# Half of the gate cells by accumulating scatters instead of one-hot products

## The chip, the cores and the metric

The kernel runs on one core of a Trainium2 chip. The metric is device time in microseconds, the median of several runs; before the change it is 2739.08 us (three runs, 2737.34 to 2743.43).

## What is computed

One encoder layer runs on two groups of tokens, 256 of the prompt and 512 of the sample (called the first and the second group here). Its attention and pooling half is not touched by the change. The other half is PEER, an expert retrieval over 128 x 128 = 16384 single-neuron experts:

```python
s = jnp.einsum('thpd,hpnd->thpn', q, keys)                 # 8 heads, 2 halves, 128 keys
top_s, top_i = lax.top_k(s, 16)
cand = top_s[:, :, 0, :, None] + top_s[:, :, 1, None, :]
best_s, best_j = lax.top_k(cand.reshape(128, 8, 256), 16)
expert = i1 * 128 + i2                                     # 16 experts per token and head
g = softmax(best_s)
act = gelu(einsum('thkd,td->thk', u[expert], x)) * g
out = einsum('thk,thkd->td', act, v[expert])
```

So each token uses 8 x 16 = 128 experts, each with a weight `g` (its gate).

## The kernel before

**Two ways of evaluating the experts.** For the second group (512 tokens, four blocks of 128) the kernel works densely. A first pass goes over the whole table `u` in 128 turns of 128 experts: TensorE multiplies a tile of `u` with all 512 tokens (`score`, 24 matmuls of 512 columns, because each operand is split in a high and a low part), ScalarE applies gelu, and the result goes to `act_scratch` in DRAM. A second pass goes over the table `v`, again 128 turns: the stored activations come back, are multiplied by the gates, split in two parts and multiplied by a tile of `v` (`combine`, 24 matmuls). For this the gates of all 512 tokens must exist as a dense array of 512 x 16384 values, `gate_scratch` in DRAM, with zero wherever a token doesn't use an expert. The first group's 256 tokens are done sparsely: 2 x 128 slots, each of which gathers one row of 8 KB (u and v) for each of 128 tokens (`gather`, an indirect DMA from POOL), multiplies and sums it on VectorE (`row_dot`), passes the sum through gelu on ScalarE (`gathered`) and adds the weighted row (`row_add`). These slots run beside both passes; `slots_of(k)` says which of them turn k takes (k from 0 to 127 is the first pass, 128 to 255 the second). Slots are two ahead in the gathers (`AHEAD`), in four buffers.

**Where the gates come from.** VectorE searches the scores (`search`, four parts, each head of each block one search; 32 in the first pass, ordered by `search_of`). The searches go block by block. When a block's eight heads are done, its weights are shifted, exponentiated and normed (`shift_block`, `exp_block`, `norm_block`), TensorE transposes the three 128 x 128 tables of first keys, second keys and weights (`turn_block`) and ScalarE copies them out (`take_block`). Then a gate step for every four tokens follows, 32 for a block and 128 in all: VectorE makes the one-hot of the first key (`hot_keys`, 128x512), ScalarE the weighted one-hot of the second key (`scale_hot`: four `Abs` of 128x128, then four `Relu`), TensorE multiplies the two for each token (`gate_step`), and ScalarE copies the 128 x 512 result to `staged` (`copy_gates`); every eight steps 2 MB of it go to `gate_scratch`. `steps_of(k)` gives one step to each of the turns 20 to 115 and four steps to each of the turns 116 to 123; in those the one-hot of the second key is made on VectorE too.

**What one turn of the first pass does.** On ScalarE: `split_tile` rounds the tile of the next turn (it waits until TensorE is done with the tile before last), `gathered`, gelu of the turn before, `scale_hot`, `copy_gates`. On VectorE: `hot_keys`, `lower_tile` (the low part of the next tile; TensorE waits for it), `use_slot` (`row_dot` of this slot, `row_add` of the one before), one part of a search. On TensorE: `score`, then `gate_step`. On SP: the load of the tile four turns ahead (512 KB), scores for the searches, the store of the activations (256 KB). Each engine takes its instructions in order; the order is written out by hand.

**The start of the second pass.** SP issues the first load of gates (1 MB, in pieces of 512 B) in turn 127, ahead of the last two stores of activations; it waits for all gate stores. The second pass reads in each turn 512 KB of `v`, 256 KB of activations, 256 KB of gates and one or two slots of 1 MB. In turns 4 to 15 of it there are two slots in each turn, in all others one.

## Time and profile before

| | us |
|---|---|
| median of three runs | 2739.08 |
| lowest, highest | 2737.34, 2743.43 |
| the profiled execution, its own time | 2744.57 |
| its span in the profile | 2742.8 |
| first pass (turns 0 to 127) | about 1055 to 1964 |
| second pass | 1969 to 2712 |

Most rows below are of a timeline: the start of an instruction in microseconds from the start of the span, its length, the engine, the line in the kernel and what it writes and reads. Lengths of neighbours overlap a little, since the engines are pipelined, so what one instruction costs is the distance between starts. A remark in square brackets says how long the engine was idle before and what it waited for. In the row of a stretch, each engine's busy time stands with its instruction count, then TensorE's granted clock (1.00 is full speed), the DMA engines' busy share and the rate of data.

### The profile page before, as it was taken

The numbers are of one execution on the slowest core, as the hardware profiler recorded it, in microseconds if no ns is written. First come the engines' busy times: TensorE is split into PE (matmuls) and PEld (weight loads), VectorE is DVE, ScalarE is ACT, GpSimd is POOL, SyncE is SP. The second block draws the span as 40 slices with busy tenths as digits, with TensorE's granted clock in tenths as the row PEclk, the third lists the DMA queues.
The fourth block names the chain that finished last, engine by engine and source line by source line (L and its number), as shares of the span: only waits on it lengthen the run. The fifth ranks groups of instructions, "written<-read, shape, count | busy, mean of one in ns | idle before, by whom it ended". The sixth has DMA issues, their size and how long they took to land.

```text
span 2742.8 us, 36197 instructions
## 1 busy us (share of the span) xinstructions
PE 2465.3 (90%) x10956; PEld 1938.4 (71%) x10956; DVE 2131.3 (78%) x3891; ACT 1234.8 (45%) x2704; POOL 571.3 (21%) x408
## 2 busy tenths in 40 slices
PE   4987888999899787899999999998878999999996
PEld 3767766666456576777777777776756888878885
DVE  4877613666388855889999999989688888888888
ACT  2332043444312142267777787777433333333333
POOL 2013104422032320011111111112122323232221
PEclk9999999999999899999999999999988999999998
DMA  6646651112032325478888888888899999999996
GB/s 275 217 163 253 255 218 62 62 62 86 23 117 101 146 78 217 136 263 309 322 299 319 298 319 309 305 304 313 318 387 347 381 382 388 384 368 380 389 382 237
DMA packets 223810, 697.60 MB, mean 254 GB/s; under 512 B 15840, under 2 KB 111456, under 8 KB 181472
## 3 DMA queue, kind: packets, MB, share of 16 engines
q1 hardware_dynamic: 165984, 367.25, 37.2%
q0 software_dynamic: 37632, 270.55, 26.0%
q10 hardware_dynamic: 20096, 58.72, 5.6%
q8 instruction: 33, 0.54, 0.1%
q14 instruction: 65, 0.53, 0.1%
HBM read 614.67 MB, written 81.79 MB: 254 GB/s over the span
## 4 chain that ended last, share of the span: by engine, by line
PE 42%; DVE 32%; DVEq 9%; DMA 8%; issue 5%; ACT 3%; SPq 1%; ACTq 1%; POOL 0%; PEldq 0%; PEld 0%
PE ps L866 21%; PE ps L557 7%; DVE g_acc L1787 5%; DVEq L1799 4%; PE ps L542 4%; DVE rows L1778 4%; DVE arena L1454 3%; DMA act_in<-act_scratch 3%; DVE hot L1741 2%; PE ps L569 2%; DMA arena<-in_weights 2%; DVE cand L1397 1%; PE ps L905 1%; DMA rows<-in_rows,pick_e 1%; DMA ring<-in_weights 1%
## 5 line engine op out<-in xcount | busy, mean ns | idle before, releaser
L1999 POOL DMA_INDIRECT rows<-in_rows,pick_e x256 | 333.4, 1302 | 1350.1 <-DVE g_acc L1787 1188.6
L1245 ACT CAST t_hi<-raw 128x1024 fp32r<-128x1024 f32 x256 | 268.8, 1050 | 545.0 <-PE ps L866 528.1
L866 PE MATMUL ps<-t_hi,c_hi 128*128 128x512 f32 x1024 | 407.4, 398 | 37.9 <-DVE t_lo L1859 33.0
L866 PE MATMUL ps<-n_hi,t_hi 128*128 128x512 f32 x1024 | 413.6, 404 | 26.4 <-DVE t_lo L1804 25.3
L866 PE MATMUL ps<-t_lo,c_hi 128*128 128x512 f32 x1024 | 404.4, 395 | 0.0
L866 PE MATMUL ps<-t_hi,c_lo 128*128 128x512 f32 x1024 | 404.1, 395 | 0.0
L866 PE MATMUL ps<-n_hi,t_lo 128*128 128x512 f32 x1024 | 401.2, 392 | 0.0
L866 PE MATMUL ps<-n_lo,t_hi 128*128 128x512 f32 x1024 | 401.0, 392 | 0.0
L1787 DVE SCALAR_TENSOR_TENSOR g_acc<-rows,small,g_acc 128x1024 f32<-128x1024 f32 x254 | 326.3, 1285 | 34.9 <-issue 9.1
L1934 POOL TENSOR_TENSOR w_lo<-ring,w_hi 128x1024 fp32r<-128x1024 f32 x76 | 189.4, 2498 | 667.2 <-ACT w_hi L998 559.9
L866 PEld LDWEIGHTS ps<-t_hi,c_hi 128*128 128x128 f32 x1024 | 196.2, 192 | 85.3 <-issue 44.5
L866 PEld LDWEIGHTS ps<-n_hi,t_hi 128*128 128x128 f32 x1024 | 193.4, 189 | 75.5 <-DVE t_lo L1804 21.2
L557 PE MATMUL ps<-n_hi,w_hi 128*128 128x512 f32 (+1 forms) x480 | 194.5, 405 | 37.4 <-POOL w_lo L1934 28.0
L866 PEld LDWEIGHTS ps<-t_lo,c_hi 128*128 128x128 f32 x1024 | 196.5, 192 | 40.8
L866 PEld LDWEIGHTS ps<-t_hi,c_lo 128*128 128x128 f32 x1024 | 195.8, 191 | 41.7
L866 PEld LDWEIGHTS ps<-n_hi,t_lo 128*128 128x128 f32 x1024 | 193.2, 189 | 42.0
L866 PEld LDWEIGHTS ps<-n_lo,t_hi 128*128 128x128 f32 x1024 | 193.7, 189 | 36.7
L542 PE MATMUL ps<-arena,ring 128*128 128x256 f32 (+1 forms) x640 | 187.4, 451 | 5.2 <-DVE arena L1666 5.1
L1778 DVE CUSTOM_DVE_ANT_0 rows<-rows,x_tok 128x1024 f32<-128x1024 f32 x144 | 175.4, 1218 | 7.7 <-DMA rows<-in_rows,pick_e 7.7
L905 PE MATMUL ps<-hot2g,hot 128*128 128x128 f32 x1024 | 142.1, 282 | 43.3 <-DVE hot L1741 24.4
L557 PE MATMUL ps<-n_lo,w_hi 128*128 128x512 f32 (+1 forms) x480 | 178.5, 372 | 0.0
L557 PE MATMUL ps<-n_hi,w_lo 128*128 128x512 f32 (+1 forms) x480 | 178.1, 371 | 0.0
(198 smaller groups left out, 4188.4 us busy)
## 6 DMA issues: line engine op xcount, KB each, us to landing
raw<-in_table SPq DMA_DIRECT2D x256, 512.0 KB, 7.2
ring<-in_weights SPq DMA_DIRECT2D x44, 2048.0 KB, 8.2
act_scratch<-act_out SPq DMA_DIRECT2D x128, 256.0 KB, 3.5
gate_scratch<-staged ACTq DMA_DIRECT2D x16, 2048.0 KB, 9.7
act_in<-act_scratch SPq DMA_DIRECT2D x128, 256.0 KB, 10.6
gate_in<-gate_scratch SPq DMA_DIRECT2D x32, 1024.0 KB, 15.6
arena<-in_weights ACTq DMA_DIRECT2D x24, 1024.0 KB, 9.4
arena<-in_weights SPq DMA_DIRECT2D x2, 2048.0 KB, 21.2
```

The costliest lines, as they stand in the source:

```text
L542: last = mm(ps[:, bank, 0:S], w[:, k, :], src[:, k, 0:S], start=(k == 0), stop=(k == n - 1))
L557: last = mm(ps[:, bank, 0:S], a, c, start=k == 0 and x == 0, stop=k == KC - 1 and x == 2, skip_group_check=True)
L569: last = mm(ps[:, bank, 0:S], a, c[:, k, 0:S], start=k == 0 and x == 0, stop=k == KC - 1 and x == 2, skip_group_check=True)
L866: last = mm(out, a, b_, start=start and x == 0, stop=stop and x == len(pairs) - 1, skip_group_check=True)
L905: last = mm(ps[:, 2 + parity, x * P:(x + 1) * P], hot1[:, parity, x, :], hot2g[:, parity, x, :], start=True, stop=True)
L1245: copy(t_hi[:, t % 2, :], raw[:, t % 4, :]).then_inc(hi_ready, 1)
L1454: V.tensor_tensor_reduce(out=dump, in0=tile, in1=c_row[:, 4 * g:4 * g + 4, :], scale=1.0, scalar=0.0, op0=ALU.mult, op1=ALU.add, accum_out ...
L1778: V.tensor_tensor_reduce(out=rows[:, t, 0:D], in0=rows[:, t, 0:D], in1=x_tok[:, x, :], scale=1.0, scalar=0.0, op0=ALU.mult, op1=ALU.add, a ...
L1787: stt(out=g_acc[:, x, :], in0=rows[:, t, D:2 * D], scalar=cf[:, t:t + 1], in1=g_acc[:, x, :], op0=ALU.mult, op1=ALU.add).then_inc(row_used, 1)
L1799: dve.drain()
L1934: G.tensor_tensor(w_lo[:, j, :], ring[:, o:o + TILE], w_hi[:, j, :].bitcast(F32), ALU.subtract).then_inc(w_lo_ready, 1)
L1999: G.indirect_dma_start(rows[:, j % 4, :], None, rows_in, bass.IndirectOffsetOnAxis(ap=pick_e[:, j:j + 1], axis=0)).then_inc(row_in[j % 4], 16)
```

## The change

Of the second group, blocks 0 and 1 keep the one-hot products: `STEPS` falls from 128 to 64. Blocks 2 and 3 get their gates by indirect DMAs that add single words into `gate_scratch` in DRAM: 256 scatters, each of one word (4 bytes) for each of 128 tokens.

- The array is first filled with zeros where the scatters go: 16 DMAs of 1 MB on SP's queue (`clear`), behind the weight loads of the second group's attention part; their source is a zeroed buffer of scores.
- The searches run in pairs, in the order of `PAIRS`. The eight pairs of blocks 2 and 3 take one head of both blocks. After such a pair VectorE computes cell addresses (`place_pair`), ScalarE takes the exponential of 32 values (`exp_pair`), and VectorE norms them (`weigh_pair`), in the turn after. Then POOL may issue its 32 scatters, up to three in an even and two in an odd turn (three before turn 24), behind the turn's gathers.
- The first 24 turns hold two parts of a search each and no slot (before: 18, and slots from turn 16 on).
- Block 0 is turned in turn 25, block 1 in turn 89. Gate steps of block 0 stand in the even turns 26 to 88 and have both one-hots made on ScalarE: eight `Abs`, one 128x512 `Relu` for the first one-hot, four `Relu` for the second; VectorE has no part in them. Gate steps of block 1 stand in the turns 90 to 121, one in each, with the first one-hot on VectorE as before. The stretch with four steps a turn is gone.
- The first pass takes 108 slots (before: 116): one in each of turns 24 to 123, two in each of turns 124 to 127. The second pass takes 148 (before: 140): two in every sixth turn from turn 3 on, 20 times, in all other turns one. ScalarE's and VectorE's second pass is written out instead of looped, and `row_add` stands right behind `row_dot` in it.
- SP issues the first load of gates behind the last store of activations, and waits for the scatters too.

```diff
-STEPS = SEQS[1] // 4
+STEPS = 2 * P // 4
 SLOTS = 2 * P
-SEARCH_BODIES = 5
-CROWDED = 29
+DENSE = 24
+TURN_AT = (25, 89)
+ZEROS = 16
 AHEAD = 2
+PAIRS = ((2, 0), (0, 0), (0, 1), (2, 1), (0, 2), (0, 3), (2, 2), (1, 0), (2, 3), (1, 1), (2, 4), (1, 2), (2, 5), (1, 3),
+         (2, 6), (2, 7))
...
-        gate_dram = scratch("gate_scratch", QUARTERS, P, P, STAGE)
+        gate_cells = scratch("gate_scratch", QUARTERS * P * P * STAGE, 1)
+        gate_dram = gate_cells.rearrange("(q p k t) a -> q p k (t a)", p=P, k=P, t=STAGE)
+        gate_zero = gate_cells.rearrange("(c p m n) a -> c p m (n a)", c=2 * ZEROS, p=P, n=2 * P)
...
+        def at_of(s):
+
+            b, n = PAIRS[s // 2]
+            return (2 + s % 2, n) if b == 2 else (b, 2 * n + s % 2)
+
+        def scattered_before(s):
+            return sum(b == 2 for b, _ in PAIRS[:s // 2])
...
         def slots_of(k):
 
-            if k < 16 or P - 4 <= k < P:
+            if k < DENSE:
                 return ()
-            if k < 4 * CROWDED:
-                return (k - 16,)
             if k < P - 4:
-                j = 100 + 2 * (k - 4 * CROWDED)
+                return (k - DENSE,)
+            if k < P:
+                j = P - 4 - DENSE + 2 * (k - P + 4)
                 return (j, j + 1)
-            if k < P + 4:
-                return (k - 12,)
-            j = 120 + 2 * (k - P - 4)
-            return (j, j + 1) if k < P + 16 else (k,)
+            v = k - P
+            j = P - DENSE + 4 + v + min((v + 2) // 6, 20)
+            return (j, j + 1) if v % 6 == 3 and v < 120 else (j,)
+
+        def starts(s):
+            return 2 * s if s < DENSE // 2 else DENSE + 4 * (s - DENSE // 2)
+
+        def search_of(k):
+
+            if k < DENSE:
+                return k // 2, (0, 1) if k % 2 == 0 else (2, 3)
+            s = DENSE // 2 + (k - DENSE) // 4
+            return (s, ((k - DENSE) % 4,)) if s < 2 * len(PAIRS) else (0, ())
+
+        def pair_of(k):
+
+            s, parts = search_of(k)
+            return scattered_before(s) if 3 in parts and s % 2 and PAIRS[s // 2][0] == 2 else None
 
         def steps_of(k):
 
-            if k < 4 * SEARCH_BODIES or k >= P - 4:
+            if k < 26 or k > 121 or (k < 90 and k % 2):
                 return ()
-            if k < 4 * CROWDED:
-                return (k - 4 * SEARCH_BODIES,)
-            return tuple(range(96 + 4 * (k - 4 * CROWDED), 100 + 4 * (k - 4 * CROWDED)))
-
-        def search_of(k):
-
-            if k < 4 * SEARCH_BODIES - 2:
-                return k // 2, (0, 1) if k % 2 == 0 else (2, 3)
-            if k < 4 * SEARCH_BODIES or k // 4 + 4 > 31:
-                return 0, ()
-            return k // 4 + 4, (k % 4,)
+            return ((k - 26) // 2,) if k < 90 else (k - 58,)
...
+                def clear(c):
+                    sp.dma_start(gate_zero[c + ZEROS], score_in[:, 1].rearrange("p a n -> p (a n)").unsqueeze(1).broadcast_to(
+                        (P, 8, 2 * P))).then_inc(zeroed, 16)
...
-                if t == 0 and 0 < i < SEARCH_BODIES:
-                    load_scores(sp, False, 2 * i + 1)
-                if t == 2 and i < SEARCH_BODIES - 1:
-                    load_scores(sp, False, 2 * i + 2)
-                if t == 0 and SEARCH_BODIES <= i < 27:
-                    load_scores(sp, False, i + 5)
-                if k == P - 1:
-                    for half in range(2):
-                        sp.wait_ge(gates_stored[half], 16 * QUARTERS // 2)
-                    load_gates(0, 0)
+                for x in range(2, 2 * len(PAIRS)):
+                    if starts(x - 1) == k:
+                        load_scores(sp, False, x)
                 if k == P // 2:
                     for t in range(4):
                         load_act(0, t)
                 if k:
                     store_act(k - 1)
             store_act(P - 1)
+            for half in range(2):
+                sp.wait_ge(gates_stored[half], 16 * STEPS // 16)
+                sp.wait_ge(scattered[half], 16 * TOPK * HEADS)
+            load_gates(0, 0)
...
             def scale_hot(s):
 
-                col = P * ((s // 32) % 2) + 4 * (s % 32)
-                if s >= 96:
-                    act.wait_ge(hot2_ready, s - 95)
-                    act.wait_ge(g_done, s - 1)
-                    for x in range(4):
-                        last = A(hot2g[:, s % 2, x, :], hot2[:, s % 2, x, :], ACT.Copy,
-                                 scale=sel_t[:, 2, col + x:col + x + 1])
-                    last.then_inc(hot2g_ready, 1)
-                    return
-                for x in range(4):
-                    A(hot2[:, s % 2, x, :], iota, ACT.Abs, bias=sel_n[:, 0, col + x:col + x + 1])
-                act.drain()
+                col = 4 * (s % 32)
                 after(act, g_done, s - 1)
                 for x in range(4):
+                    if s < 32:
+                        A(hot1[:, s % 2, x, :], iota, ACT.Abs, bias=sel_n[:, 0, col + x:col + x + 1])
+                    A(hot2[:, s % 2, x, :], iota, ACT.Abs, bias=sel_n[:, 1, col + x:col + x + 1])
+                act.drain()
+                if s < 32:
+                    A(hot1[:, s % 2], hot1[:, s % 2], ACT.Relu, bias=ones[:, 0:1], scale=-1.0)
+                for x in range(4):
                     last = A(hot2g[:, s % 2, x, :], hot2[:, s % 2, x, :], ACT.Relu,
-                             bias=sel_t[:, 2, col + x:col + x + 1], scale=sel_n[:, 1, col + x:col + x + 1])
+                             bias=sel_t[:, 2, col + x:col + x + 1], scale=sel_n[:, 2, col + x:col + x + 1])
                 last.then_inc(hot2g_ready, 1)
...
+            def exp_pair(p):
+
+                act.wait_ge(pair_shifted, p + 1)
+                v = sel[:, 2, P + 32 * (p % 2):P + 32 * (p % 2) + 32]
+                A(v, v, ACT.Exp).then_inc(pair_exped, 1)
...
+            def place_pair(p):
+
+                o, n = P + 32 * (p % 2), 32 * p
+                keys1, keys2, v = (sel[:, x, o:o + 32] for x in range(3))
+                stt(out=keys1, in0=keys1, scalar=float(P), in1=keys2, op0=ALU.mult, op1=ALU.add)
+                V.tensor_copy(gsum[:, 0:2], v.rearrange("p (h k) -> p h k", k=TOPK)[:, :, 0])
+                dve.drain()
+                tt(v.rearrange("p (h k) -> p h k", k=TOPK), v.rearrange("p (h k) -> p h k", k=TOPK),
+                   gsum[:, 0:2].unsqueeze(2).broadcast_to((P, 2, TOPK)), ALU.subtract).then_inc(pair_shifted, 1)
+                for x in range(2):
+                    ts(cell[:, n + TOPK * x:n + TOPK * (x + 1)], keys1[:, TOPK * x:TOPK * (x + 1)], float(STAGE),
+                       token[:, x:x + 1], ALU.mult, ALU.add)
+
+            def weigh_pair(p):
+
+                o, n = P + 32 * (p % 2), 32 * p
+                v = sel[:, 2, o:o + 32].rearrange("p (h k) -> p h k", k=TOPK)
+                dve.wait_ge(pair_exped, p + 1)
+                V.tensor_reduce(gsum[:, 2:4], v, AX.X, ALU.add)
+                dve.drain()
+                V.reciprocal(gsum[:, 2:4], gsum[:, 2:4])
+                dve.drain()
+                tt(cell_g[:, n:n + 32].rearrange("p (h k) -> p h k", k=TOPK), v,
+                   gsum[:, 2:4].unsqueeze(2).broadcast_to((P, 2, TOPK)), ALU.mult).then_inc(pair_ready, 1)
...
             for k in range(P):
-                i, t = k // 4, k % 4
-                block = (i + 1 - SEARCH_BODIES) // 8 + 2 if (i + 1 - SEARCH_BODIES) % 8 == 0 else None
-                if block is not None and t == 0:
-                    shift_block(block % 2, 1)
                 for s in steps_of(k):
-                    hot_keys(s)
+                    if s >= 32:
+                        hot_keys(s)
                 lower_tile(k + 1)
                 for j in slots_of(k):
                     if j == 0:
                         dve.wait_ge(x_in, 32)
                     use_slot(j)
+                if k and pair_of(k - 1) is not None:
+                    weigh_pair(pair_of(k - 1))
+                if k + 1 in TURN_AT:
+                    norm_block(0, 1, 2 + TURN_AT.index(k + 1), sel[:, 2, 0:P], sel_ready)
                 m, parts = search_of(k)
+                b, h = at_of(m)
                 for part in parts:
-                    search(False, m, P * (m // 8 % 2) + 16 * (m % 8), part)
-                if block is not None and t == 2:
-                    half = block % 2
-                    norm_block(half, 1, block, sel[:, 2, half * P:(half + 1) * P], sel_ready)
+                    if (b, h, part) == (1, 0, 3):
+                        dve.wait_ge(sel_turned, 1)
+                    search(False, m, P + 16 * (2 * (scattered_before(m) % 2) + b - 2) if b >= 2 else 16 * h, part)
+                if pair_of(k) is not None:
+                    place_pair(pair_of(k))
+                if k + 2 in TURN_AT:
+                    shift_block(0, 1)
...
+            def scatter(n):
+
+                b, h = n // TOPK % 2, n // (2 * TOPK)
+                if n % (2 * TOPK) == 0:
+                    pool.wait_ge(pair_ready, h + 1)
+                if n % TOPK == 0:
+                    after(pool, scattered[b], 16 * TOPK * h)
+                G.indirect_dma_start(gate_cells, bass.IndirectOffsetOnAxis(ap=cell[:, n:n + 1], axis=0),
+                                     cell_g[:, n:n + 1], None, compute_op=ALU.add).then_inc(scattered[b], 16)
...
+                known = 2 * TOPK * sum(pair_of(x) is not None for x in range(min(k, P)))
+                pace = 3 if k < DENSE or k % 2 == 0 else 2
+                while sent < known and (pace > 0 or k == P - 1):
+                    scatter(sent)
+                    sent += 1
+                    pace -= 1
```

What stands on ScalarE in a turn of the first pass, before (one whole turn; `hot2` and `hot2g` are the one-hot of the second key without and with the weight, `t_hi` the rounded tile):

```order
L1250 ACTIVATE act_out<-ps 128x512
L1270 ACTIVATE hot2<-cst,sel_n 128x128 x4
L1274 ACTIVATE hot2g<-hot2,sel_t,sel_n 128x128 x4
L1284 COPY staged<-ps 128x128x4
L1245 CAST t_hi<-raw 128x1024
L1309 ACTIVATE small<-small 128x1
L1311 ACTIVATE small<-small,pick_g 128x1
L1250 ACTIVATE act_out<-ps 128x512
L1270 ACTIVATE hot2<-cst,sel_n 128x128 x4
L1274 ACTIVATE hot2g<-hot2,sel_t,sel_n 128x128 x4
L1284 COPY staged<-ps 128x128x4
```

And in the changed kernel in an even turn of 26 to 88 (`hot1` is the one-hot of the first key), up to the next turn's start:

```order
L1287 ACTIVATE act_out<-ps 128x512
L1301 ACTIVATE hot1<-cst,sel_n 128x128
L1302 ACTIVATE hot2<-cst,sel_n 128x128
L1301 ACTIVATE hot1<-cst,sel_n 128x128
L1302 ACTIVATE hot2<-cst,sel_n 128x128
L1301 ACTIVATE hot1<-cst,sel_n 128x128
L1302 ACTIVATE hot2<-cst,sel_n 128x128
L1301 ACTIVATE hot1<-cst,sel_n 128x128
L1302 ACTIVATE hot2<-cst,sel_n 128x128
L1305 ACTIVATE hot1<-hot1,cst 128x512
L1307 ACTIVATE hot2g<-hot2,sel_t,sel_n 128x128 x4
L1317 COPY staged<-ps 128x128x4
```

Between gelu and the last `Relu` there were eight instructions of 128x128; now there are twelve and one of 128x512. The odd turns have none of them.

On POOL, the end of the program before: all 256 gathers follow each other.

```order
L294 DMA score_in<-score_scratch 128x256
L1934 TENSOR_TENSOR w_lo<-ring,w_hi 128x1024 x3
L294 DMA score_in<-score_scratch 128x256
L1934 TENSOR_TENSOR w_lo<-ring,w_hi 128x1024 x3
L1999 DMA rows<-in_rows,pick_e 128x2048 x256
```

In the changed kernel, from the first scatters (`cell` holds addresses, `cell_g` the weights) over the first gathers of the slots:

```order
L2056 DMA gate_scratch<-cell_g,cell 8388608x1 x56
L2045 DMA rows<-in_rows,pick_e 128x2048
L2056 DMA gate_scratch<-cell_g,cell 8388608x1 x3
L2045 DMA rows<-in_rows,pick_e 128x2048
L2056 DMA gate_scratch<-cell_g,cell 8388608x1 x2
L2045 DMA rows<-in_rows,pick_e 128x2048
L2056 DMA gate_scratch<-cell_g,cell 8388608x1 x3
L2045 DMA rows<-in_rows,pick_e 128x2048 x6
L2056 DMA gate_scratch<-cell_g,cell 8388608x1 x3
L2045 DMA rows<-in_rows,pick_e 128x2048
L2056 DMA gate_scratch<-cell_g,cell 8388608x1 x2
L2045 DMA rows<-in_rows,pick_e 128x2048
```

Between two gathers now stand two or three scatters, over most of the first pass.

## Rows read from the trace of the kernel before

**Rows 1.** Stretches: length, PE PEld DVE ACT POOL busy, clock, share, GB/s.

```profile
1190.00:1842.00 652.00, 623.05 (x3030) 511.58 (x3031) 597.53 (x1271) 510.61 (x1242) 95.91 (x95) 1.00 0.84 308
1842.00:1943.00 101.00, 85.64 (x481) 70.98 (x480) 87.95 (x120) 77.35 (x219) 20.33 (x15) 1.00 0.83 311
2015.00:2107.00 92.00, 67.46 (x240) 52.10 (x239) 74.03 (x94) 29.43 (x64) 21.51 (x19) 0.83 0.98 368
2107.00:2383.00 276.00, 275.45 (x1204) 227.88 (x1204) 245.59 (x304) 98.09 (x200) 81.43 (x51) 0.99 1.02 381
```

**Rows 2.** Timeline of ScalarE: start, length, instruction; gelu in early turns.

```profile
1141.23 0.59 ACT L1250 ACTIVATE act_out<-ps 128x512 f32<-128x512 f32 x1
...
1153.70 0.59 ACT L1250 ACTIVATE act_out<-ps 128x512 f32<-128x512 f32 x1
```

**Rows 3.** The same, the last gelu of the first pass.

```profile
1964.16 0.60 ACT L1250 ACTIVATE act_out<-ps 128x512 f32<-128x512 f32 x1 [3.84 <-PE ps L866]
```

**Rows 4.** Timeline of VectorE over four turns of the first pass.

```profile
1568.11 1.22 DVE L1804 TENSOR_TENSOR t_lo<-raw,t_hi 128x1024 fp32r<-128x1024 f32 x1
...
1571.77 0.17 DVE L1429 COPY sel<-pair 128x16 f32<-128x16 f32 x1
...
1574.20 0.69 DVE L1741 TENSOR_TENSOR hot<-sel_t,cst 128x512 f32<-128x512 f32 x1
...
1591.34 0.42 DVE L1418 TENSOR_TENSOR cand<-best 128x256 f32<-128x256 f32 x1
...
1595.02 0.69 DVE L1741 TENSOR_TENSOR hot<-sel_t,cst 128x512 f32<-128x512 f32 x1
1595.62 1.22 DVE L1804 TENSOR_TENSOR t_lo<-raw,t_hi 128x1024 fp32r<-128x1024 f32 x1
```

**Rows 5.** Timeline of ScalarE, one of these turns.

```profile
1575.39 1.05 ACT L1245 CAST t_hi<-raw 128x1024 fp32r<-128x1024 f32 x1 [0.47 <-PE ps L866]
1577.21 0.20 ACT L1309 ACTIVATE small<-small 128x1 f32<-128x1 f32 x1 [0.77 <-DVE small L1778]
...
1577.68 0.58 ACT L1250 ACTIVATE act_out<-ps 128x512 f32<-128x512 f32 x1
1578.16 1.27 ACT L1270 ACTIVATE hot<-cst,sel_n 128x128 f32<-128x128 f32 x4
1579.50 1.66 ACT L1274 ACTIVATE hot2g<-hot,sel_t,sel_n 128x128 f32<-128x128 f32 x4
```

**Rows 6.** Timeline of TensorE, gate steps of two turns.

```profile
1581.66 1.06 PE L905 MATMUL ps<-hot2g,hot 128*128 128x128 f32 x8
...
1588.08 1.05 PE L905 MATMUL ps<-hot2g,hot 128*128 128x128 f32 x8
```

**Rows 7.** Groups of ScalarE instructions, 1190 to 1835 us.

```profile
L1293 ACT ACT_TABLE_LOAD x3 | 3.8, 1283 | 0.1
```

**Rows 8.** Chain that ended last, where the second pass starts.

```profile
1956.10 10.46 DMA gate_in<-gate_scratch
...
1968.94 6.16 PE ps L866 x17
```

**Rows 9.** DMA issues in the first pass: count, us to landing.

```profile
rows<-in_rows,pick_e POOLq DMA_INDIRECT x57, 6.0
```

**Rows 10.** The same in the second pass.

```profile
rows<-in_rows,pick_e POOLq DMA_INDIRECT x50, 9.3
```

**Rows 11.** DMA queues while the first gates load: packets, MB, engine share.

```profile
q1 hardware_dynamic: 3077, 3.69, 83.4%
```

**Rows 12.** Timeline of VectorE, one turn of the second pass.

```profile
2205.21 1.22 DVE L1859 TENSOR_TENSOR t_lo<-raw,t_hi 128x1024 fp32r<-128x1024 f32 x1
...
2210.65 1.22 DVE L1859 TENSOR_TENSOR t_lo<-raw,t_hi 128x1024 fp32r<-128x1024 f32 x1
```

**Rows 13.** Timeline of TensorE, the end of the second pass.

```profile
2712.95 0.39 PE L866 MATMUL ps<-t_hi,c_lo 128*128 128x512 f32 x1
```

**Rows 14.** The page: the gathers on POOL.

```profile
L1999 POOL DMA_INDIRECT rows<-in_rows,pick_e x256 | 333.4, 1302 | 1350.1 <-DVE g_acc L1787 1188.6
```

167 lines of the change are left out of this document (83 added, 84 removed).

## The prediction

> **What bounds the kernel now.** I read the stretches first [rows 1], then three timelines of the same four turns of the first pass, then the chain at the border of the passes, then the second pass.
>
> In the first pass (1190 to 1842 us) TensorE is busy 623 of 652 us and VectorE 598 of 652. Which of them bounds? Four turns of VectorE's timeline [rows 4] run from the low part at 1568.11 to the one at 1595.62: 27.5 us, 6.88 a turn. Low part, `row_dot` and `row_add` take 3.66 (1568.11 to 1571.77), the one-hot 0.60 (1595.02 to 1595.62), so the four parts of a search take 27.5 - 4 x 4.26 = 10.5 (the third 3.68, the fourth 2.43, the first two 4.4 together). The instructions follow each other without a gap. TensorE needs only 6.42 for a turn with a gate step (1581.66 to 1588.08 [rows 6]), of which the 24 matmuls are 5.44 (a turn of the second pass [rows 12]) and the gate step 1.0. So VectorE bounds the turns with a search, TensorE those without. Before the slots start, two turns with one search last 12.47 (1141.23 to 1153.70 [rows 2]).
>
> From 1842 to 1943 stand the eight turns with four gate steps each, 11 to 12 us a turn. The last gelu is at 1964.16 [rows 3]. The second pass starts at 1968.94, after the gates' load of 10.46 us that SP issued at 1956.10 [rows 8]. It ends at 2713.3 [rows 13]: 744 us for 128 turns, of which 128 x 5.44 = 696 are TensorE's. The rest is lost mostly in the twelve turns with two slots: from 2015 to 2107 TensorE is busy 67 of 92 us at 368 GB/s. In the steady stretch behind it TensorE is full, but so is the DMA, share 1.02 at 381 GB/s [rows 1]. A turn moves 0.52 + 0.26 + 0.26 + 1.05 = 2.10 MB in 5.44 us, 385 GB/s.
>
> **The change, part by part.** I count from the gelu of turn 15 at 1153.70, up to which both kernels do the same (but for one pair's small work, counted below).
>
> *Turns 16 to 23*, each with half a search and no slot: 4 x 12.47 = 50 us. Pairs 0 and 1 add small VectorE operations, seven or eight each; the trace has none of just that size but a 128x16 copy at 0.17 (1571.77 [rows 4]), so with drains about 1.9 a pair, 4 in all (bounds 2 and 8). That gives 1207.6.
>
> *Turns 24 and 25*, slot and search, no gate step: 2 x 3.66 + 4.4 + 1.5 for the block's norm = 13 us: 1220.8.
>
> *Turns 26 to 89*, a gate step in every even turn. VectorE loses the one-hot: 4 x 3.66 + 10.5 = 25.1 for four turns. TensorE needs 2 x 6.42 + 2 x 5.44 = 23.7. But the one-hots now queue up on ScalarE behind a wait for TensorE. In an even turn ScalarE may start `split_tile` only when `score` of the turn before is done; from there [rows 5]: rounding 1.05, the two small ones of the slot 0.47 (1577.21 to 1577.68), gelu 0.48, four `Abs` with the drain 1.34, four more at (1.27 - 0.39) / 3 = 0.29 each 1.2, one 128x512 `Relu` 0.5 (as gelu, 1577.68 to 1578.16), four `Relu` 1.66: 6.7, and 0.1 for the hand-over. TensorE is done with this turn's `score` after 5.44 and waits 1.3 for them. Then gate step 1.0 and the odd turn's `score` 5.44, whose end opens the next even turn. 6.8 + 1.0 + 5.44 = 13.2 for two turns, against 13.76 before and 11.9 of TensorE's own. Behind the waiting gate step the next `score` is queued, so nothing hides it. VectorE (12.55) fits beside it. 32 x 13.2 = 422. If the chain is hidden in some way, VectorE's 12.55 stays: 21 less; if VectorE's and ScalarE's waits add, the old 13.76: 18 more. In four of the even turns (32, 48, 64, 80) an exponential stands before the one-hots, with a table load of 1.283 before and behind it [rows 7]: 2.8 each on that path, 11 in all; taking block 0 1 more. The last gelu of the stretch comes at 1655.
>
> *Turns 90 to 103*: as before, 14 x 6.88 = 96, block 1's turn 2.5, two pairs at 3.5 (their exponential and VectorE's 1.9, less some slack) 7: 1761. *Turns 104 to 121*: gate step, slot, no search, VectorE 4.3, TensorE's 6.42: 18 x 6.42 = 116: 1876. *122, 123*: 11. *124 to 127* with two slots: VectorE 1.1 + 2 x 2.5 = 6.2; data 0.79 + 2.1 = 2.9 MB at 385 GB/s 7.5; I take 7.1: 28. The last gelu comes at 1916 instead of 1964: 48 us earlier, all of it where 32 gate steps used to be crowded.
>
> *The scatters.* POOL's issue of a gather takes 1.3 us [rows 14]; two or three scatters more between two gathers are 2.5 x 1.3 = 3.3, with the gather 4.6 of a turn of 6.6, and a gather has some 17 us from issue to use against 6.0 to landing [rows 9]. On the DMA engines a scatter is 128 packets, 8 for each engine. No row shows a packet of 4 bytes, nor an accumulating one. The nearest: while gates load, 3077 packets take 83.4% of 16 engines for 13 us, 56 ns each, at a mean of 1.2 KB [rows 11]. 20 packets a turn on each engine are 1.1 us of 6.6, a share of 0.17 on top of 0.84 [rows 1]: just full. So I take nothing. Downward there is no gain. Upward, 8 packets of 8 KB land in 6.0; if 8 of a scatter filled their queue for as long, 256 x 6 = 1540 us would bound the pass, far outside.
>
> *The zeros*: 16 MB on SP's queue during the second group's attention, where the DMA engines are mostly idle; each 2 to 4 MB stand behind a load of weights that is already on its way, and the next waits a head's work. Nothing, bounds 0 and 5.
>
> *The border.* SP now loads the gates behind the last store of activations, which waits for the last gelu: 0.6 + 0.5 for the store's issue + 10.46 + 2.4 (1966.56 to 1968.94 [rows 8]) = 14 us from gelu to second pass, instead of 4.8: +9. It starts at 1930. TensorE idles meanwhile.
>
> *The second pass.* Twenty turns with two slots instead of twelve. A second slot is 2.5 on VectorE, and in six turns there is room for it. For the DMA it is 1.05 MB on a full machine. 128 x 2.10 + 12 x 1.05 + 3.1 (final operands) = 284 MB at 385 GB/s are 738; measured 744. Now 128 x 2.10 + 20 x 1.05 + 3.1 = 292.5 MB: 760 + 6 = 766, +22. The bounds for the twenty are nothing (engines with room left: 704 + 8) and 3.8 each (92 us for ten turns in the stretch from 2015, less 5.44) for all: 788.
> The Trainium skill, "DMA: Bandwidth & Descriptors", section Specifications, gives a core's HBM limit as about 358 GB/s. The 276 us at 381 GB/s [rows 1] disagree. By that rule the second pass would take 292.5 / 358 = 817 us and the change would be slower by 30; I go by the row.
>
> **The sum.** -48 + 9 + 22 = -17. The profiled execution took 2744.57 us, 5 above the median; it would be 2727.5, and against the median of 2739 that is 2722.
>
> **The rivals.**
> *A, slower: the scatters are POOL's or its queue's bound.* One place, the line of POOL in turns 24 to 117: it decides from the point where 1.3 + 2.5 c exceeds the turn of 6.6, c = 2.1 us a scatter. For it: a gather waits in order behind the scatters, and no row shows their price; against: the 1.3 of a gather's issue. At c = 2.5 a turn takes 7.55, 0.95 more in some 85 turns: +81, 2803 us.
> The Trainium skill, same page, section "Anatomy of one DMA — SWDGE (gpsimd) path", puts about 2.0 us of fixed cost on each such DMA. No run here shows it for scatters; if it were all taken in sequence, c = 2.0 would stand just below the point.
> *B, faster: the second pass has room.* If the 385 GB/s are only what TensorE asks for, the twenty slots cost a third: 40 less, 2682. Against: share 1.02, and gathers that land in 9.3 us there [rows 10] instead of 6.0.
> *C, the gain is eaten.* The chain on ScalarE gives nothing (+18) and the double turns cost 3.8 each (+22): 2762; with one of the two, about 2742.
>
> **How the numbers follow.** Forecast 0.45, A 0.20, B 0.15, C 0.20. The range 2685 to 2800 leaves out most of B's far side and A's worse half. The measurement can tell about 0.2% (5.5 us) from no change. Of the forecast's 0.45 some 0.06 is no change, of C's 0.20 0.07; A and the rest of C are slower. Faster 0.54, within 0.2% 0.13, slower 0.33.
>
> **What would show it.** Even turns of 26 to 89: TensorE waits about 1.3 us before the gate step for ScalarE's `Relu`, two turns 13.2. A last gelu near 1916, and some 14 us without matmuls behind it, with the gates' load in the chain. In the second pass a share above 1 all the way, turns of 5.44 broken after each double turn. POOL still idle for `row_add` in the first pass; if instead it is never idle and VectorE waits for rows, A is right. I am wrong altogether if the turns 104 to 121 are not near 6.42, or if the first group's or the attention's time moves.

## The result and the profile after

| | before | after |
|---|---|---|
| median, us | 2741.61 | 2745.15 |
| profiled execution, its own time and span | 2744.57, 2742.8 | 2743.88, 2742.1 |
| last gelu of the first pass | 1964.16 | 1938.00 |
| first matmul of the second pass | 1968.94 | 1955.10 |
| end of the last matmul | 2718.8 | 2717.9 |

The ratio is 1.0018, 95% interval 1.001 to 1.0025: slower by 0.2%, less than one can use, where 0.6% faster had been forecast. The forecast of 2722 was wrong. The two profiled executions are 0.7 us apart, so their stretches can be set against each other: the first pass ends 26.2 us earlier (forecast 48), the border costs 12.3 more (17.1 from gelu to matmul instead of 4.8; forecast 9), and the second pass 13.0 more (762.8 instead of 749.8; forecast 22). Together -0.9. The profiled execution of before is 3 us above the median of its twenty and that of after 1.3 below, so the 3.5 us between the medians are not to be found in these stretches.

First two stretches of [rows 1] in the kernel after (length, then busy time of PE, PEld, DVE, ACT, POOL, the granted clock, the DMA share, GB/s):

```profile
1190.00:1842.00 652.00, 573.69 (x2646) 471.02 (x2645) 534.31 (x1175) 435.32 (x1041) 438.92 (x279) 0.97 0.88 279
...
2107.00:2383.00 276.00, 261.99 (x1130) 209.32 (x1130) 241.65 (x305) 99.48 (x204) 61.32 (x54) 1.00 1.02 380
```

TensorE was busy 623 of the 652 us and is now busy 574; VectorE fell from 598 to 534. Neither is full, so something else sets the turns. POOL rose from 96 to 439. In the second pass TensorE lost 13 of 276 us at the same DMA rate.

ScalarE's timeline of one even turn, to be read beside [rows 5]:

```profile
1362.57 1.05 ACT L1282 CAST t_hi<-raw 128x1024 fp32r<-128x1024 f32 x1 [4.48 <-PE ps L897]
...
1363.99 0.58 ACT L1287 ACTIVATE act_out<-ps 128x512 f32<-128x512 f32 x1
1364.47 0.39 ACT L1301 ACTIVATE hot<-cst,sel_n 128x128 f32<-128x128 f32 x1
...
1366.97 0.73 ACT L1305 ACTIVATE hot<-hot,cst 128x512 f32<-128x512 f32 x1
1367.60 1.64 ACT L1307 ACTIVATE hot2g<-hot,sel_t,sel_n 128x128 f32<-128x128 f32 x4
```

ScalarE is idle 4.48 us until TensorE has finished `score`, and then works 6.7 us to the last `Relu` (1362.57 to 1369.24). TensorE's timeline shows who waits for it; the gate steps of two turns and the first matmul of `score` behind the first of them; the second stands behind a pair's exponential:

```profile
1369.37 1.15 PE L937 MATMUL ps<-hot2g,hot 128*128 128x128 f32 x8 [1.46 <-ACT hot2g L1307]
1370.28 0.48 PE L897 MATMUL ps<-n_hi,t_hi 128*128 128x512 f32 x1
...
1385.85 1.77 PE L937 MATMUL ps<-hot2g,hot 128*128 128x128 f32 x8 [4.40 <-ACT hot2g L1307]
```

Between them ScalarE did this:

```profile
1376.11 1.05 ACT L1282 CAST t_hi<-raw 128x1024 fp32r<-128x1024 f32 x1 [4.49 <-PE ps L897]
1377.18 1.28 ACT L1343 ACT_TABLE_LOAD   x1
1378.47 0.23 ACT L1343 ACTIVATE sel<-sel 128x32 f32<-128x32 f32 x1
1378.72 1.28 ACT L1349 ACT_TABLE_LOAD   x1
```

The chain that the prediction described is there: two turns take 13.52 us (1362.57 to 1376.11), 0.3 over the forecast of 13.2. A turn with an exponential makes TensorE wait 4.40. The gate step behind it takes 1.77 instead of 1.15, and from 1384 to 1394 the granted clock is 0.83, a stretch spent partly at the lower of the two levels (1.2 and 2.4 GHz).

POOL's groups between 1226 and 1680 (count, busy us and mean ns, idle before them):

```profile
L2056 POOL DMA_INDIRECT gate_scratch<-cell_g,cell x125 | 228.3, 1826 | 63.0 <-issue 36.9 <-DVE cell_g L1830 26.1
L2045 POOL DMA_INDIRECT rows<-in_rows,pick_e x64 | 71.0, 1109 | 92.4 <-DVE g_acc L1844 77.4 <-issue 14.9
```

A scatter holds POOL for 1.83 us and 0.3 more of issue, 2.1 in all, not the 1.3 that the sum went by. That is the point from which rival A decides: 1.4 for the gather and 2.5 x 2.1 are 6.7 of a turn of 6.8. A gather takes 7.7 us from issue to landing here, against 6.0 [rows 9].

The chain that ended last, at the border, answers to [rows 8]:

```profile
1938.00 0.59 ACT act_out L1287
...
1939.11 13.62 DMA gate_in<-gate_scratch
...
1955.10 6.92 PE ps L897 x20
```

The step is the one forecast. The load takes 13.62 instead of 10.46.

In the second pass VectorE's timeline, from the low part (`t_lo`) in a turn with two slots, shows where a double turn's price arises (compare [rows 12], one turn of 5.44):

```profile
2554.09 1.22 DVE L1915 TENSOR_TENSOR t_lo<-raw,t_hi 128x1024 fp32r<-128x1024 f32 x1
...
2561.47 1.22 DVE L1915 TENSOR_TENSOR t_lo<-raw,t_hi 128x1024 fp32r<-128x1024 f32 x1
...
2566.33 1.22 DVE L1915 TENSOR_TENSOR t_lo<-raw,t_hi 128x1024 fp32r<-128x1024 f32 x1
...
2570.70 1.28 DVE L1844 SCALAR_TENSOR_TENSOR g_acc<-rows,small,g_acc 128x1024 f32<-128x1024 f32 x1 [1.41 <-ACT small L1351]
...
2572.51 1.22 DVE L1915 TENSOR_TENSOR t_lo<-raw,t_hi 128x1024 fp32r<-128x1024 f32 x1
```

From one `t_lo` to the next the six turns take 7.38, 4.86, 6.19, 5.44, 5.61, 5.44: 34.92 instead of 32.64, so a double turn costs 2.3 us. One turn of VectorE alone is 4.86. It could make up the 7.38 in the following turns, but two turns later it loses 1.41 waiting for `gathered` on ScalarE. ScalarE was late by its own order:

```profile
2568.64 1.05 ACT L1282 CAST t_hi<-raw 128x1024 fp32r<-128x1024 f32 x1 [4.22 <-PE ps L897]
2569.59 0.61 ACT L1293 CAST c_hi<-act_in 128x512 fp32r<-128x512 f32 x1
2570.11 0.20 ACT L1349 ACTIVATE small<-small 128x1 f32<-128x1 f32 x1
2570.38 0.29 ACT L1351 ACTIVATE small<-small,pick_g 128x1 f32<-128x1 f32 x1
```

The coefficient, 0.5 us of work, stands behind the tile's rounding, which waits 4.22 us for TensorE's `combine` to free the tile buffer.

### The profile page after: what moved, and what is told of

The parts are those of the page before. It is cut to its first block, busy times and chain, and to the rows that moved or that the text cites. A ratio compares the mean times of both kernels' runs of the same rounds, so it can differ in the third digit from the quotient of the medians.

```text
span 2742.1 us, 34124 instructions
## 1 busy us (share of the span) xinstructions
PE 2401.4 (88%) x10438; PEld 1873.8 (68%) x10438; DVE 2054.3 (75%) x3817; ACT 1140.9 (42%) x2430; POOL 982.4 (36%) x665
## 4 chain that ended last, share of the span: by engine, by line
PE 48%; DVE 21%; ACT 8%; DMA 7%; DVEq 5%; issue 5%; ACTq 4%; SPq 1%; POOL 0%; PEldq 0%; PEld 0%
PE ps L897 26%; PE ps L588 7%; PE ps L573 4%; DVE arena L1492 3%; ACTq L1350 3%; DMA act_in<-act_scratch 2%; DVEq L1856 2%; PE ps L937 2%; PE ps L600 2%; DVE g_acc L1844 2%; DVE rows L1835 2%; DVE t_lo L1915 2%; DMA arena<-in_weights 2%; ACT hot L1302 1%; DMA ring<-in_weights 1%
## 5 line engine op out<-in xcount | busy, mean ns | idle before, releaser
L2045 POOL DMA_INDIRECT rows<-in_rows,pick_e x256 | 289.2, 1129 | 779.7 <-DVE g_acc L1844 719.3
L2056 POOL DMA_INDIRECT gate_scratch<-cell_g,cell x256 | 454.1, 1774 | 157.5 <-DVE cell_g L1830 81.6
L1835 DVE CUSTOM_DVE_ANT_0 rows<-rows,x_tok 128x1024 f32<-128x1024 f32 x256 | 312.1, 1219 | 9.6 <-DMA rows<-in_rows,pick_e 9.6
L1861 DVE TENSOR_TENSOR t_lo<-raw,t_hi 128x1024 fp32r<-128x1024 f32 x129 | 158.5, 1228 | 100.6 <-ACT t_hi L1282 97.4
## 6 DMA issues: line engine op xcount, KB each, us to landing
gate_scratch<-score_in SPq DMA_DIRECT2D x16, 1024.0 KB, 11.9
```

Of the source, the lines that this page charges most:

```text
L1835: V.tensor_tensor_reduce(out=rows[:, t, 0:D], in0=rows[:, t, 0:D], in1=x_tok[:, x, :], scale=1.0, scalar=0.0, op0=ALU.mult, op1=ALU.add, a ...
L1861: tt(t_lo[:, K % 2, :], raw[:, K % 4, :], t_hi[:, K % 2, :].bitcast(F32), ALU.subtract).then_inc(lo_ready, 1)
L2045: G.indirect_dma_start(rows[:, j % 4, :], None, rows_in, bass.IndirectOffsetOnAxis(ap=pick_e[:, j:j + 1], axis=0)).then_inc(row_in[j % 4], 16)
L2056: G.indirect_dma_start(gate_cells, bass.IndirectOffsetOnAxis(ap=cell[:, n:n + 1], axis=0), cell_g[:, n:n + 1], None, compute_op=ALU.add).t ...
```

## The experiments

Each began from the kernel after. "Stretch" is gelu(25) to gelu(89), 443.9 us before and 456.3 after. "Second pass" runs from its first matmul to the end of its last. Intervals are 95%. The medians belong to several sessions, in which the kernel before had 2738.2 to 2741.6 us; kernels are therefore compared by their ratios to it. Each stretch comes from one trace. Where an edit doesn't touch it, the stretch of after took 456.2 to 458.2 us in seven traces (after, e4, e5, e9, e10, e13, e15) and the second pass 761.8 to 767.6 in eight (after, e1, e2, e3, e4, e6, e8, e11), so less than 2 and 6 us say nothing there.

### The one-hots on ScalarE a turn earlier (e1)

```
-                for s in steps_of(k):
+                for s in hots_of(k):
                     scale_hot(s)
```
`hots_of(k)` gives block 0's step (k-25)//2 in the odd turns 27 to 87 (step 0 stays in turn 26, block 1's stay where they were).

> The changed kernel, but ScalarE makes the one-hots of block 0 in the odd turn before their gate step (the first of them still in turn 26). Theory 1, the queue on ScalarE sets the turns 26 to 89: two turns take 13.53 us now, of which 1.46 is TensorE's wait for the last Relu, and four pairs' exponentials add some 4.4 each. With the one-hots a turn ahead both leave the path, two turns fall to VectorE's 12.6 to 12.9, the stretch from 456 to about 410, the kernel by 40 to 46 us, to about 0.985 of before. Theory 2, the scatters (1.77 us each on POOL, and their packets) slow this stretch: the turns stay near 13.5 and the time where it is, 1.002 of before.

2732.86 us, ratio 0.998 (0.9968 to 0.9992). TensorE's wait for `hot2g` is gone (57.5 us between 1226 and 1660 before the edit, 2.1 with it), but the stretch is 438.4, only 17.9 less where some 46 had been expected. Its waits between 1226 and 1660 (engine and line waiting, for whom: us, times, longest) name the next one:

```profile
...
POOL rows L2051 <- DVE g_acc L1850: 65.1, 17, 6.5
...
PE ps L903 <- DVE t_lo L1867: 36.6, 18, 5.6
...
DVE rows L1841 <- DMA rows<-in_rows,pick_e: 30.0, 15, 4.4
```

TensorE waits for VectorE, and VectorE for gathered rows that come too late. POOL's timeline says why (start, length, instruction, idle before it):

```profile
1304.30 1.93 POOL L2051 DMA_INDIRECT rows<-in_rows,pick_e  x1 [0.30 <-issue]
1306.53 1.75 POOL L2062 DMA_INDIRECT gate_scratch<-cell_g,cell  x1 [0.30 <-issue]
1308.58 1.56 POOL L2062 DMA_INDIRECT gate_scratch<-cell_g,cell  x1 [0.30 <-issue]
1310.45 1.00 POOL L2051 DMA_INDIRECT rows<-in_rows,pick_e  x1 [0.30 <-issue]
1311.76 1.58 POOL L2062 DMA_INDIRECT gate_scratch<-cell_g,cell  x1 [0.30 <-issue]
1313.64 2.22 POOL L2062 DMA_INDIRECT gate_scratch<-cell_g,cell  x1 [0.30 <-issue]
1316.16 1.75 POOL L2062 DMA_INDIRECT gate_scratch<-cell_g,cell  x1 [0.30 <-issue]
1318.22 1.97 POOL L2051 DMA_INDIRECT rows<-in_rows,pick_e  x1 [0.30 <-issue]
```

From the gather at 1304.30 to the one at 1318.22, two turns, POOL never waits for another engine: 13.9 us for two gathers and five scatters, when two turns without scatters take 12.7 on average (405.5 for 64, e8 below). So it goes until a pair's 32 scatters are out; the 65.1 us in which POOL waits for `row_add` lie in the turns behind them. This is rival A's mechanism, hidden in the kernel after by ScalarE's queue.

### The scatters left out (e3), and both edits (e8), and a slower pace (e11)

```
-                G.indirect_dma_start(gate_cells, ..., compute_op=ALU.add).then_inc(scattered[b], 16)
```
In e3 this goes, with the waits for it; e8 has e1's edit too. Both outputs lack the gates of blocks 2 and 3. e11 keeps all scatters and e1's edit, and issues two in every turn from 24 on:
```
-                pace = 3 if k < DENSE or k % 2 == 0 else 2
+                pace = 3 if k < DENSE else 2
```

> The changed kernel without the 256 scatters (the gates of blocks 2 and 3 are missing from the output). Theory 1b: behind ScalarE's queue the scatters are hidden but for a little, POOL's lead in the gathers takes them up; the turns 26 to 89 stay at 13.5 for two, and only the last four turns and the first load of gates gain: 3 to 8 us less, 1.000 of before. Rival A of the prediction (the scatters bound the pass): 25 us less or more, under 0.993.

> The kernel of e1 (one-hots of block 0 a turn ahead) without the 256 scatters, so the gates of blocks 2 and 3 are missing from the output. Theory 1b: e1 gained 18 us in turns 26 to 89 instead of 46 because POOL is then the bound, 2.5 scatters at 1.8 + 0.3 and a gather at 1.3 + 0.3 are 6.9 us a turn, and VectorE waits for rows (30 us). Without them two turns fall to 12.6, the stretch from 438 to about 410, and with the other turns the kernel by 30 to 40 us against e1, to 0.985 of before. Rival: VectorE and its hand-over with ScalarE are the bound in e1, and the stretch stays at 430 or more.

> The kernel of e1 (one-hots of block 0 a turn ahead) with two scatters in every turn from 24 on, instead of three and two by turns: a pair's 32 scatters then fill its 16 turns evenly, 2 x 2.1 + 1.6 = 5.8 us of POOL a turn. Theory 1b (POOL is the bound in e1): 5.8 is under VectorE's 6.3, and most of the 38 us between e1 and e8 in turns 26 to 89 come back: 20 to 30 us less than e1, 0.988 to 0.991 of before. Rival, the packets themselves slow the gathers: no better than e1, 0.998.

| | stretch, us | median, us | ratio (interval) |
|---|---|---|---|
| after | 456.3 | 2745.15 | 1.0018 (1.001 to 1.0025) |
| e3, no scatters | 458.3 | 2738.77 | 0.9993 (0.998 to 1.0006) |
| e1, one-hots ahead | 438.4 | 2732.86 | 0.998 (0.9968 to 0.9992) |
| e8, both | 405.5 | 2687.73 | 0.9804 (0.9782 to 0.9826) |
| e11, e1 with two a turn | 410.3 | 2703.43 | 0.9863 (0.9843 to 0.9883) |

Taking the scatters alone away gives nothing in the stretch, ScalarE's order alone 17.9, both 50.8. Two limits stand one behind the other, and the first hides the second. e11 does all the scatters and gets 28.1 of the last 32.9 us back. Between 1226 and 1640 a gather takes 8.4 us from issue to landing in it, as in e1 (8.5; 6.9 without scatters, e8), while VectorE's wait for rows falls from 30.0 to 2.0 us: what held e1 was the time at which POOL issued the gathers, not how long the DMA took for them. Its scatters and gathers between 1226 and 1640:

```profile
L2062 POOL DMA_INDIRECT gate_scratch<-cell_g,cell x120 | 210.1, 1751 | 59.7 <-issue 35.4 <-DVE cell_g L1836 24.4
L2051 POOL DMA_INDIRECT rows<-in_rows,pick_e x64 | 88.0, 1376 | 58.2 <-DVE g_acc L1850 46.3 <-issue 11.9
```

In place of the full 6.9 us a turn, 2.5 x 2.1 + 1.6, POOL now needs 5.8, 2 x 2.05 + 1.7, and waits for `row_add` now and then between the scatters too.

### The first one-hot back on VectorE (e2)

`hot_keys(s)` is called for all steps again, and ScalarE's `Abs` and 512-wide `Relu` for block 0 are dropped.

> The changed kernel, but the one-hot of the first key is made on VectorE in block 0 too (one part undone). ScalarE's work ahead of the gate step is 1.8 us shorter, VectorE has 0.6 more in every even turn. Theory 1: the chain falls from 13.53 to 11.7, VectorE's own 12.55 + 0.6 = 13.15 for two turns takes its place, 0.4 less in 32 pairs of turns, and the exponentials stay: 8 to 15 us less, 0.997 of before. Theory 2 (scatters): nothing, or 0.6 x 32 = 19 us more if VectorE is what they slow.

2739.27, ratio 0.9996 (0.9983 to 1.0008); the stretch is 449.6, 6.7 less, under the 8 to 15 expected. Several pairs of turns fall from 13.52 to 11.85, but the four turns round a pair's exponential take 31.4 to 34.2 us instead of 31.6. It agrees with e1 in direction: it shortens ScalarE's queue, and lengthens VectorE's.

### The pairs' exponentials without a table load (e6)

```
-                A(v, v, ACT.Exp).then_inc(pair_exped, 1)
+                A(v, v, ACT.Copy).then_inc(pair_exped, 1)
```
It leaves out the exponential, so blocks 2 and 3 don't get their weights.

> The changed kernel with a copy in place of the exponential of each pair (weights of blocks 2 and 3 wrong), so that no table is loaded for it. Theory 1: each of the four pairs in turns 26 to 89 costs 4.4 us of ScalarE's queue, of which 2.9 are the two loads and the rest TensorE's slow restart behind the longer wait; with the four pairs outside that stretch at 1 to 2 us each, 15 to 22 us less, 0.995 of before. Rival: the loads are hidden, the cost of a pair is VectorE's small operations: under 5 us less.

2742.21, ratio 1.0011 (1.0 to 1.0023): a miss. Eight of the ten table loads between 1226 and 1680 are gone, 8 x 1.283 = 10.3 us, and the stretch falls by 7.4 only. The four exponentials do not share in it alike. ScalarE's timeline at the first two of them:

```profile
1263.61 0.23 ACT L1343 ACTIVATE sel<-sel 128x32 f32<-128x32 f32 x1 [0.37 <-DVE sel L1815]
...
1374.20 0.23 ACT L1343 ACTIVATE sel<-sel 128x32 f32<-128x32 f32 x1 [2.19 <-DVE sel L1815]
```

The third is like the first and the fourth like the second. In the kernel after, the four turns round an exponential (30 to 33, for one) take 31.6 us, 4.5 over two ordinary pairs of turns (27.0). At the first and third the `Copy` waits 0.4 us for VectorE's pair work, and the turns take 27.6: 4.0 of the 4.5 are gone with the two loads, 2.4 of them in TensorE's wait (4.39 to 2.04) and the rest behind it. The gate step takes 1.15 again instead of 1.67, and the granted clock from 1269 to 1279 is 1.00. At the second and fourth the `Copy` waits 2.2 us for VectorE, which had worked beside the table load; TensorE still waits 3.85 and 4.04, and the turns take 31.8 and 31.2. Behind the second, from 1380 to 1390, the clock is 0.74 and the gate step 2.07. So theory 1's account, two loads and TensorE's slow restart, holds in two of the four, and VectorE's work stands in their place in the other two.

The gain does not reach the end of the pass: from gelu(25) to the last gelu it is 714.5 us, after 714.8. Turns 114 to 117 take 31.1 instead of 25.4 and turns 122 to 127 43.1 instead of 38.3. Between 1800 and 1850 VectorE waits 12.5 us for gathered rows while POOL has nothing between its DMAs but issue; in the kernel after there is no such wait there. It looks like POOL's limit again; no run of e6 with fewer scatters a turn tests it.

### The gates' load ahead of the last stores (e4)

```
+                if k == P - 1:
+                    for half in range(2):
+                        sp.wait_ge(gates_stored[half], 16 * STEPS // 16)
+                        sp.wait_ge(scattered[half], 16 * TOPK * HEADS)
+                    load_gates(0, 0)
```

> The changed kernel, but SP issues the first load of gates in turn 127 ahead of the last two stores of activations, as before. Theory 1: the gates are complete since turn 122, so the load of 13.6 us starts 11 us earlier and TensorE's gap of 17 us at the border of the passes shrinks to about 6: 10 to 12 us less, 0.998 of before. Rival: the load then competes with the gathers for which the last four turns already wait (9 us landings), and they lose what the border gains: no change.

2738.97, ratio 1.0004 (0.999 to 1.0017). From the last gelu to the second pass it is 11.9 us instead of 17.1: 5.2 less, half of what was expected. The load is issued at 1922.29, 10.2 us ahead of the last gelu instead of 1.1 behind it, but beside the gathers and stores of the last turns it takes 19.76 us instead of 13.62. The rival was right that they compete, but it is the load that loses: turns 122 to 127 take 38.5 us, after 38.3.

### What sets the second pass (e5, e9, e10, e13, e15)

e5 moves `row_add` of a single slot to the end of VectorE's turn, so that it never waits for ScalarE. e9 puts the gates' product before the second slot. e10 loads half of each tile of the second table and leaves out the rest:
```
-                    sp.dma_start(raw[:, t, :], table[bass.ds(4 * i + (t + 4), 1), :, D:2 * D]...
+                    sp.dma_start(raw[:, t, 0:D // 2],
+                                 table[bass.ds(4 * i + (t + 4), 1), :, D:D + D // 2]...
```
e13 lets ScalarE compute the first slot's coefficient before the roundings:
```
+                gathered(slots[0] - 1, (slots[0] - 1) % 4)
                 if not (last and t == 3):
                     split_tile(32 + i, t + 1)
                     split_coef(4 * i + (t + 1), t + 1)
-                for j in slots_of(P + 4 * i + t):
+                for j in slots[1:]:
                     gathered(j - 1, (j - 1) % 4)
```
e15 is e13 and e10 together.

> The changed kernel, but in the second pass row_add stands at the end of VectorE's turn again (behind the low parts and the product with the gates; in double turns the first of two stands behind the low part). Theory 3, VectorE's order sets the loss of the double turns: row_add waits for ScalarE (75.8 us in all) and delays the low part, so each double turn costs TensorE 2.3 us; without that wait most of the 20 x 2.3 goes: 25 to 45 us less, 0.987 to 0.993 of before. Theory 4, the bytes on a full DMA set it: 292.5 MB at no more than 393 GB/s are 744 against 763 us now, and gathers are issued later than now; 0 to 15 us less, 0.997 to 1.002.

> The changed kernel, but in the double turns of the second pass VectorE makes the product with the gates before the second slot. Theory 5, the second slot delays that product and with it ScalarE's high part and the next low part (ScalarE waits 59 us for the product in the pass): each double turn costs less than its 2.3 us, 10 to 30 us less in all, 0.991 to 0.998 of before. Theory 4, the bytes: nothing. Theory 6, it is the distance of 7.38 us between two low parts on VectorE, whatever the order of the rest: nothing either.

> The changed kernel, but in the second pass only the first half of each tile of v is loaded (0.26 MB less a turn; the other half of the tile is what lay there, so the sample output is wrong). Theory 4, the bytes on a full DMA set the second pass: 763 us fall to TensorE's 696 plus little, 40 to 60 less, 0.98 to 0.985 of before. Theories 5 and 6, VectorE's order: the pass stays within 10 us of 763, 0.998 to 1.002.

> The changed kernel, but in the second pass ScalarE computes the coefficient of the turn's first slot before it waits for TensorE (ahead of split_tile and split_coef) instead of behind. Theory 7: what makes a double turn cost 2.3 us is that VectorE has no slack left, since its row_add stands ahead of the low parts and waits for a coefficient that ScalarE computes only behind the tile's rounding (59 us in 600). With that wait gone the low part comes about 2 us before it is due, just what a double turn adds: the pass falls from 763 to 715 to 735, 0.982 to 0.991 of before. Theory 6 (the distance of 7.38 between low parts costs this whatever else stands there): nothing.

> The reordered second pass (the first slot's coefficient ahead of the tile's and the coefficients' rounding) with half of each tile of the second table loaded (the other half is stale, so the output is the sum with a wrong half; work on the engines is the same). With the reordering alone the second pass took 750.2 us, VectorE waited 37.0 us for activations from memory between 2100 and 2650, at 389 to 391 GB/s and a DMA share of 1.04. Theory: the DMA engines' bytes are the next bound there. With 0.26 MB less a turn the waits for activations fall below 10 us, the share is 0.97 or less, and the second pass takes 720 to 735 us, the kernel about 2705. Rival: the waits come from the order in which transfers are issued and not from the bytes; they stay above 25 us and the second pass stays at 745 to 752, the kernel at 2725 to 2732.

| | second pass, us | median, us | ratio (interval) |
|---|---|---|---|
| after | 762.8 | 2745.15 | 1.0018 (1.001 to 1.0025) |
| e5, add last | 782.4 | 2766.18 | 1.0106 (1.0048 to 1.0164) |
| e9, product first | 764.2 | 2743.2 | 1.0011 (0.9998 to 1.0025) |
| e10, half tiles | 760.7 | 2741.06 | 1.0002 (0.9989 to 1.0015) |
| e13, coefficient first | 750.2 | 2729.45 | 0.9971 (0.9958 to 0.9983) |
| e15, both | 724.5 | 2700.36 | 0.9863 (0.9846 to 0.9879) |

e5 was slower: the buffers come free later, so the gathers go out later, and VectorE waits for rows instead, 53.3 us between 2100 and 2650 against 2.8. e9 took 25 us of ScalarE's wait for the product away (43.3 to 18.5 us) and changed nothing, so that wait cost nothing. e10 did nothing either (2.1 us is within the spread), though the DMA had room. Its stretches:

```profile
2100.00:2400.00 300.00, 283.78 (x1216) 226.89 (x1217) 264.40 (x335) 107.22 (x222) 66.78 (x59) 0.99 0.96 338
2400.00:2650.00 250.00, 238.55 (x1034) 191.34 (x1033) 222.09 (x279) 88.76 (x186) 56.75 (x50) 1.00 0.97 344
```

In after, the wait for ScalarE's coefficient leads VectorE's list between 2100 and 2650:

```profile
DVE g_acc L1844 <- ACT small L1351: 53.4, 57, 2.5
```

In e13 it is gone, and another stands there:

```profile
DVE act_in L1930 <- DMA act_in<-act_scratch: 37.0, 18, 5.4
...
PE ps L897 <- DVE t_lo L1917: 23.1, 24, 3.1
```

Six turns now take about 33 us, and every other six 36 to 38, with a turn of 8 us or more in them that waits for a load of activations. e15 tells whether that is bytes or order. The same view of e15, where `act_in` waits for no DMA at all, and its stretches:

```profile
DVE c_lo L1788 <- ACT c_hi L1294: 17.5, 37, 2.2
...
PE ps L898 <- DVE t_lo L1918: 3.7, 17, 1.2
```

```profile
2100.00:2400.00 300.00, 298.52 (x1306) 244.11 (x1305) 284.45 (x355) 116.46 (x239) 70.09 (x63) 1.00 1.00 362
2400.00:2650.00 250.00, 247.69 (x1084) 202.49 (x1083) 234.62 (x293) 94.44 (x194) 58.03 (x52) 1.00 1.00 361
```

It is bytes: the second pass took 724.5, in the range of the theory and far from the rival's 745 to 752. (The share of 0.97 or less that the theory also named did not come; it is 1.00, with TensorE full too.) Fewer bytes alone give 2.1 us, the order alone 12.6, both 38.3; TensorE is then busy 298.5 of 300 us.

The two limits are nearly equal over a part of the pass. From 2400 to 2650 neither edit alone gives anything: TensorE is busy 238.4 us in after, 237.3 in e13, 238.6 in e10 and 247.7 in e15. The row of after:

```profile
2400.00:2650.00 250.00, 238.35 (x1032) 190.88 (x1031) 222.01 (x279) 88.69 (x187) 57.08 (x50) 1.00 1.04 390
```

And of e13:

```profile
2400.00:2650.00 250.00, 237.26 (x1025) 192.38 (x1025) 225.30 (x282) 92.03 (x188) 57.53 (x51) 0.99 1.04 389
```

### The repairs together (e14)

e1's edit, two scatters a turn, the gates' load ahead and the coefficient first: e11, e4 and e13.

> Four edits together on the changed kernel: one-hots of block 0 a turn ahead, two scatters in every turn, the first load of gates ahead of the last two stores, ScalarE's coefficients first in the second pass. If theories 1, 1b and 7 hold and add up: 18 + 25 + 8 + 35 = 86 us less than 2743, about 2657, 0.970 of before. Rival: the DMA, with 292.5 MB in the second pass at no more than 393 GB/s, holds it at 744: about 2685, 0.979.

2689.29 us, ratio 0.9823 (0.9809 to 0.9838), the full computation: by the ratios some 53 us less than the kernel after and 49 less than before. The sum of the theories, 2657, was out of reach; the rival's 2685 came near, and its bound for the second pass, 744, is near the 749.9. The second pass is 749.9, as in e13, and the stretch 410.3, as in e11. The gains of these two add, because they lie one after another in time. The border's was lost: 20.5 us from the last gelu (1887.40) to the second pass, against 11.9 in e4. The chain there (start, length, what):

```profile
1890.55 1.73 POOL gate_scratch L2065
...
1892.59 3.04 DMA gate_scratch<-cell_g,cell
...
1895.71 9.84 DMA gate_in<-gate_scratch
```

At two a turn the last scatter is only issued when the first pass is over, and the gates' load has to wait for it. The load itself, with the first pass over, takes 9.84 us. A pace of two where the chain of TensorE wants the room and three behind it would be the next version; it was not run.

## Why the prediction was wrong, point by point

**What was right.** Turns 16 to 25: gelu(25) at 1223.25, forecast 1220.8 (gelu(15) and gelu(23) came later than forecast, each held up on ScalarE by a pair's exponential, and the next turn made it up). Turns 104 to 121, "TensorE's 6.42": 6.41. The chain's links in turns 26 to 89, and the turn that starts them: a wait of 1.46 where 1.3 was said. The extra wait at the border, and its place. The zeros cost nothing: the first gelu of this group is at 1061.60, before 1061.11.

**The step that failed in the first pass** is the sum of turns 26 to 89: "the last gelu of the stretch comes at 1655"; it came at 1679.56. The stretch took 456.3 instead of 434.2, and this is all of the 22 us by which the last gelu missed 1916 (+2.5 before it, -2.6 behind it). Its mechanism held; terms of its sum were too small. The ordinary pair of turns was 13.52, not 13.2: 32 x 0.32 = 10. ScalarE's part of it, from the tile's rounding to the gate step, was the 6.8 of the forecast (1362.57 to 1369.37), though the 512-wide `Relu` took 0.63 to the next instruction and not 0.5. TensorE's part was 6.74 (1369.37 to 1376.11) and not 1.0 + 5.44: the gate step took 0.91, but from the first matmul of `score` (1370.28) to ScalarE's start behind it it was 5.83. "2.8 each" for the exponential was 4.5, as the gate step and the `score` behind it were slower too: 4 x 1.7 = 7. The remaining 5 lie mostly at block 1's own exponential (its two table loads stand at 1661 and 1663), where the last four turns took 31.4 us, 4.4 over two ordinary pairs; this stretch had nothing for it, and its turning was priced, at 2.5, only behind turn 89. The stretch came out longer than before's 443.9: removing the one-hot from VectorE bought nothing, as rival C said. The second pass came out 9 us better than forecast and hid part of this in the total.

**The scatters' price** was wrong without hurting: 2.1 us on POOL, not 1.3. "So I take nothing" held only because ScalarE's queue was as slow. e1 against e8 prices them at 32.9 us in turns 26 to 89 as soon as that queue is gone. Rival A's point of decision, c = 2.1, was well placed: the scatters' c came out at it, 6.7 us of POOL in turns of 6.8, and decided once the turns were to be shorter.
The Trainium skill, "DMA: Bandwidth & Descriptors", section "Anatomy of one DMA — SWDGE (gpsimd) path", puts about 2.0 us of fixed cost on each DMA that POOL issues, most of it for the confirmation that the data has landed and not for the set-up. That is not the time on POOL's own timeline, 1.83 + 0.3 for a scatter and 1.11 + 0.3 for a gather in the same stretch, so that the first is near 2.0 proves nothing. A scatter of 512 bytes in all took 3.04 from issue to landing in the chain of e14.

**The border**: 17.1 instead of 14, for the load of 13.62 that had been taken at 10.46. It was 19.76 in e4, beside the last gathers and stores, and 9.84 in e14, behind them; why it was longer here than before was not tested.

**The second pass**: +13.0, forecast +22, from a cause that was half the story, and from a wrong row. [rows 13] was not the end, nor is the 2712 of the table ahead: before's last matmul starts at 2718.39, so its second pass was 749.8 and not 744. The forecast length of 766 was near the 762.8, but the difference was not, and the nearness is in part luck. The step that failed is "a second slot is 2.5 on VectorE, and in six turns there is room for it. For the DMA it is 1.05 MB on a full machine". There was room on VectorE, but it could not be used, since the slot's coefficient stood behind a wait on ScalarE: a double turn costs 2.3 us, 46 for the twenty. The bytes alone are not that price, nor is the order alone: with fewer bytes nothing measurable comes back, with the other order 12.6, with both 38.3. Before, the turns with two slots stood side by side: from the fifth `t_lo` of the pass on, these twelve took 109.1 us, 44 more than 12 x 5.44, a wait of 4.16 for activations among it, and so some 40. So twenty spread cost 6 more than twelve crowded. The largest part of the other 7 is one wait near the start of the pass, on VectorE:

```profile
2006.18 0.69 DVE L1928 TENSOR_TENSOR act_in<-act_in,gate_in 128x512 f32<-128x512 f32 x1 [8.64 <-DMA act_in<-act_scratch]
```

It was 4.16 before, at about the same place; what makes the rest is not shown. The DMA's bytes are real as a limit, 12.6 us behind the first one, and the share could not tell which of the two was in front: from 2107 to 2383 it was 1.02 in both kernels, and from 2400 to 2650 it was 1.04 at 389 to 390 GB/s in after and in e13.

**The rivals.** C came nearest: its figure for one half of it, "about 2742", and the half that came was the chain on ScalarE; the double turns did not cost 3.8 each. A's mechanism was there and hidden. B fell: with the order mended and all bytes kept (e13) the pass still took 750.2 us; only with fewer bytes too (e15) was there room.

## What to carry to other kernels

When work moves off the bounding engine, lay the receiving engine's queue out in order, behind the wait at its head. Here 0.5 us of work behind a 4.2 us wait cost 12.6 us in one pass, and one-hots behind the same kind of wait took the whole gain of turns 26 to 89 in the other. When a removed cost brings nothing, remove it once more together with the next suspect: scatters 0, order 18, both 51; bytes 2, order 13, both 38. A share of the DMA above 1 in two kernels says that a limit is near, not that it is the one that ends last. And look at each place by itself before taking a mean: e6's 7.4 us were 4.0 at two of four places and nothing at the others.

## What the runs showed of the hardware

- An accumulating scatter of single words took POOL 1.77 us on average over the whole run (256 of them) with 0.3 between two. A gather took 1.01 without scatters around it (e8) and 1.38 among them (e11), up to 1.97 (e1).
- A gather of 1 MB took 6.9 us from issue to landing without scatters (e8) and 8.4 to 8.5 among them, at a pace of two or of two and a half a turn alike (e11, e1).
- The DMA engines moved 389 to 391 GB/s at a share of 1.04 when they were the limit (e13), and 362 at a share of 1.00 when TensorE was (e15). The Trainium skill, "DMA: Bandwidth & Descriptors", section Specifications, has about 358 GB/s for a core, a stack's 716 divided by two cores; here one core ran alone and passed it, and the measurement decides.
- In ScalarE's queue two table loads of 1.28 us were worth 4.0 us where nothing else was late, 1.6 of it in TensorE's slower work behind the longer wait (granted clock 0.85 from 1274 to 1284 with them, 1.00 from 1269 to 1279 without), and nothing where VectorE's work of the same length had gone on beside them (e6).
